# Column groups for sums of squares, and transposes in place of products with the identity

## The reference

```python
def l2norm(x):
    xf = x.astype(jnp.float32)
    return xf * lax.rsqrt(jnp.sum(xf * xf, axis=-1, keepdims=True) + EPS)
...
    o = gated_delta_rule_chunked(heads(l2norm(q)), heads(l2norm(k)), heads(v.astype(jnp.float32)),
                                 heads(g), heads(beta))
```

```python
    d = jnp.where(lower, b[..., :, None] - b[..., None, :] + li[..., None, :], -jnp.inf)
    m_inter = b + m_prev[..., None]
    m_out = jnp.maximum(m_inter, jnp.max(d, axis=-1))
    dw = jnp.exp(d - m_out[..., None])
```

## Time and profile before

| | |
|---|---|
| median of 3 executions | 2449.74 us (2447.25 to 2452.32) |
| the profiled execution | 2448.92 us |
| its span in the profile | 2447.1 us |
| TensorE busy | 2233.5 us (91%) |
| VectorE busy | 1082.5 us (44%) |
| ScalarE busy | 589.0 us (24%) |
| granted TensorE clock, mean | 0.963 of full |
| loads | 266 GB/s on the mean |

### The profile page before, as it was taken

The page is one execution under the profiler, slowest core; times in us unless marked ns, Lnnn a source line. Parts: engine busy times, 40 slices in busy tenths (PEclk is TensorE's granted clock), DMA queues, the critical chain, the costliest instruction groups (busy, mean ns, idle before and its releaser), DMA issues.

```text
span 2447.1 us, 31932 instructions
## 1 busy us (share of the span) xinstructions
PE 2233.5 (91%) x12988; PEld 1448.7 (59%) x12988; DVE 1082.5 (44%) x2393; ACT 589.0 (24%) x1306; POOL 58.4 (2%) x88
## 2 busy tenths in 40 slices
PE   8999999999999999999998997888899999988876
PEld 7888869946865798467764333333568743433332
DVE  4765458883464588543433222222324342222222
ACT  4331513001243220031622211111314422111111
POOL 0010000001000000002000000000002000000000
PEclk9999999999999999999998999999899989999998
DMA  8221244496933645935248999999943469999997
GB/s 305 104 78 69 85 143 170 170 370 210 324 121 106 228 166 206 343 131 172 103 180 360 427 428 427 428 427 428 355 144 111 199 246 428 427 427 427 428 427 309
DMA packets 141343, 650.67 MB, mean 266 GB/s; under 512 B 7018, under 2 KB 13466, under 8 KB 116608
## 3 DMA queue, kind: packets, MB, share of 16 engines
q1 hardware_dynamic: 138768, 641.47, 66.4%
q0 software_dynamic: 2416, 7.02, 1.2%
HBM read 647.16 MB, written 1.31 MB: 265 GB/s over the span
## 4 chain that ended last, share of the span: by engine, by line
PE 63%; DMA 22%; DVE 10%; ACT 3%; issue 1%; DVEq 0%; ACTq 0%
PE ps L106 61%; DMA wring<-in_w_gate 5%; DMA wring<-in_w_up 5%; DMA AR<-in_w_gate 5%; DMA wring<-in_w_down 4%; DVE wring L129 2%; PE ps L109 2%; DMA AR<-in_w_up 2%; DVE AR L125 2%; DVE AR L129 1%; ACT AR L115 1%; ACT L115 1%; ACT HT L115 1%; DVE wring L125 1%; DVE AR L120 1%
## 5 line engine op out<-in xcount | busy, mean ns | idle before, releaser
L106 PE MATMUL ps<-HT,wring 128*128 128x256 f32 (+1 forms) x2848 | 532.3, 345 | 5.7 <-DVE wring L125 4.0
L106 PEld LDWEIGHTS ps<-HT,wring 128*128 128x128 f32 x2848 | 466.6, 193 | 63.5 <-issue 6.6
L106 PE MATMUL ps<-wring,AR 128*32 128x512 f32 (+3 forms) x1312 | 339.1, 616 | 21.9 <-DMA wring<-in_w_down 13.7
L106 PE MATMUL ps<-wring,MN 128*32 128x512 f32 (+1 forms) x1376 | 219.6, 642 | 49.3 <-DMA wring<-in_w_gate 32.0
L115 ACT ACTIVATE AR<-ps 128x128 f32<-128x128 f32 (+6 forms) x234 | 94.6, 404 | 651.9 <-PE ps L106 596.0
L106 PEld LDWEIGHTS ps<-wring,AR 128*32 128x32 f32 (+1 forms) x1312 | 131.8, 152 | 181.5 <-issue 165.5
L141 DVE COPY HT<-ps 128x512 f32<-128x512 f32 x64 | 44.3, 692 | 417.6 <-PE ps L106 417.6
L106 PE MATMUL ps<-AR 128*128 128x128 f32 (+6 forms) x1368 | 195.2, 404 | 15.3 <-DMA AR<-in_w_down 8.2
L106 PEld LDWEIGHTS ps<-wring,MN 128*32 128x32 f32 (+1 forms) x1376 | 62.3, 122 | 196.8 <-issue 105.6
L125 DVE TENSOR_TENSOR AR<-ps,AR 128x512 f32<-128x512 f32 (+4 forms) x200 | 100.5, 503 | 151.5 <-PE ps L106 90.6
L106 PEld LDWEIGHTS ps<-AR 128*128 128x128 f32 (+4 forms) x1368 | 135.9, 175 | 52.0 <-issue 30.5
(11 more groups left out here) (178 smaller groups left out, 2140.9 us busy)
## 6 DMA issues: line engine op xcount, KB each, us to landing
wring<-in_w_up SPq DMA_DIRECT2D x40, 2048.0 KB, 41.8
wring<-in_w_gate SPq DMA_DIRECT2D x38, 2048.0 KB, 44.5
wring<-in_w_down SPq DMA_DIRECT2D x38, 2048.0 KB, 43.2
wring<-in_w_ada SPq DMA_DIRECT2D x24, 2048.0 KB, 11.5
wring<-in_ffn_w_up SPq DMA_DIRECT2D x20, 2048.0 KB, 7.9
AR<-in_w_down SPq DMA_DIRECT2D x20, 2048.0 KB, 46.7
AR<-in_w_gate SPq DMA_DIRECT2D x20, 2048.0 KB, 36.0
wring<-in_w_in SPq DMA_DIRECT2D x18, 2048.0 KB, 9.9
```

The lines of the kernel that those rows point to most:

```text
L106: return Ins(self.eng and self.eng.matmul(out, lhs, rhs, start=start, stop=stop), None)
```

## The change

Three places of the program are edited.

1. The strip is 63 columns wide, and a piece's four matmuls write to the four groups of 32 partitions of the bank, each with 32 weight columns. Head f = 4j + r stands on partition 32r + j; the other rows get only zeros. The roots are then formed over all 128 partitions of `RN`.
2. The roots are transposed whole, two transposes of 128x128. VectorE copies the keys' 16 numbers per token into `rq` in the order of the heads, between its two masks `causal(2)` and `causal(3)`, under the new key `"rk"`. TensorE waits for that, and spreads each key head by transposes of the number repeated 128 times, two a head. The queries' numbers are read later, as before.
3. In the linear memory's `"weigh"` the matmul with the identity is a transpose of the same operand.

```diff
-    parts["strip"] = np.broadcast_to(np.arange(31) == 15, (128, 31))
+    parts["strip"] = np.broadcast_to(np.arange(63) == 31, (128, 63))
...
-                    e.matmul(pss[0:16, 0:256], C("strip", 31)[:, 15 - f:31 - f], SQ[f], f == 0, f == 15).then_inc(done, ("sum", f))
+                    r, j = 32 * (f % 4), f // 4
+                    e.matmul(pss[r:r + 32, 0:256], C("strip", 63)[:, 31 - j:63 - j], SQ[f], j == 0, j == 3).then_inc(done, ("sum", f))
...
             e.wait_ge(vect, "rn")
             for m in range(2):
-                ins = e.transpose(ps[:, m * 16:m * 16 + 16], RN[0:16, tok(m)], IDENT[0:16, 0:16])
+                ins = e.transpose(ps[:, tok(m)], RN[:, tok(m)], IDENT)
             ins.then_inc(done, "rq")
+            rq = sm("rq", 2, 16)
+            e.wait_ge(vect, "rk")
             for h in range(4):
                 ps = bank(e, PA, ("rk", h))
                 for j in range(2):
                     hd = 2 * h + j
-                    ins = e.matmul(ps[:, 256 * j:256 * j + 256], bc(IDENT[0:16, 8 + hd:9 + hd], 128), RN[0:16, :], True, True)
+                    for m in range(2):
+                        ins = e.transpose(ps[:, 256 * j + 128 * m:256 * j + 128 * m + 128], bc(rq[:, m, 8 + hd:9 + hd], 128), IDENT)
                 ins.then_inc(done, ("rk", h))
...
-                            ins = e.matmul(ps[:, k * 128:k * 128 + 128], bc(cb[:, k, 4 * d + hd:4 * d + hd + 1], 128), IDENT, True, True)
+                            ins = e.transpose(ps[:, k * 128:k * 128 + 128], bc(cb[:, k, 4 * d + hd:4 * d + hd + 1], 128), IDENT)
...
-            v.tensor_scalar(RN[0:16, :], PA["squares"][0:16, 0:256], 1e-6, None, ADD).then_inc(done, "squares")
+            v.tensor_scalar(RN, PA["squares"][:, 0:256], 1e-6, None, ADD).then_inc(done, "squares")
             PA.free("squares", (done, "squares"))
-            root_inverse("rn", RN[0:16, :], done)
+            root_inverse("rn", RN, done)
             conv(17)
-            root_step("rn", RN[0:16, :], RN1[0:16, :], RN2[0:16, :], act, done, "rn")
-            for q in range(2, 4):
-                causal(q)
+            root_step("rn", RN, RN1, RN2, act, done, "rn")
+            causal(2)
+            v.wait_ge(mm, "rq")
+            by_head = pair(PB["rq"][:, 0:256]).rearrange("p m (g c) -> p m c g", g=4)
+            rows4 = rq.rearrange("p m (c g) -> p m c g", g=4)
+            v.tensor_copy(rows4[:, :, 2:4, :], by_head[:, :, 2:4, :]).then_inc(done, "rk")
+            causal(3)
```

More of the change, by code:

```diff
@@ L1886, in gdn @@
                 scaled_keys(h)
-            v.wait_ge(mm, "rq")
-            v.tensor_scalar(rq.rearrange("p a b -> p (a b)"), PB["rq"][:, 0:32], 128.0 ** -0.5, None, MUL).then_inc(done, "rq")
+            v.tensor_scalar(rows4[:, :, 0:2, :], by_head[:, :, 0:2, :], 128.0 ** -0.5, None, MUL).then_inc(done, "rq")
             PB.free("rq", (done, "rq"))
@@ L2734, in gdn @@
                 a.activation(DT[q], DT[q], ACT.Exp, scale=-1.0).then_inc(done, ("decay", q))
-            root("rn", RN[0:16, :], RN1[0:16, :], vect, done)
+            root("rn", RN, RN1, vect, done)
             memory_squares(0)
```

## The result

The changed kernel takes 2437.49 us (median of 7), the kernel before 2448.70 (median of 7): a ratio of 0.9957, with a 95% interval of 0.9947 to 0.9967, 11.2 us or 0.43% less. A second series gave 2438.15 beside 2448.31, 10.2 us less. The profiled execution took 2435.96 us, with a span of 2434.2 against 2447.1.

What follows compares the result with a forecast made beforehand. TensorE holds 63% of the chain of waits; TensorE and VectorE are both nearly full at the mixer's roots. 3.7 + 0.25 - 0.2 + 2.7 = 6.45 us less gives 2443.3 us, range 2440.0 to 2447.5.

Steps and rivals of the forecast that it cites:

- The sums: Delta-rule mixer: four grouped matmuls take 0.60 us instead of 1.83; three of four pieces count, 3.7 us at the roots.
- the fourth: Last piece of sums before the roots: its gain only makes TensorE wait longer for the roots.
- the wide operations on VectorE: Roots over 128 partitions instead of 16: priced at nothing, at worst 0.4 us more.
- The keys by transposes: Keys' roots: sixteen transposes replace eight matmuls of 5.44 us; products start after 5.43 us instead of 5.70, gain 0.25 us.
- a sign of failing: At the keys' roots: the prediction fails if TensorE waits longer than 2.5 us for the copy and the keys.
- The clock there: Keys' products: the clock falls as now and returns a few microseconds into them; 0.2 us taken off.
- the transposes would keep it up: Rival, 15%, at the keys' roots: transposes of 128 rows hold the full clock, 1.2 to 1.4 us more gained, 2442.0.
- The rows that I had set against the rule of the Trainium skill: Stretches at 138 to 140 and 1188 to 1190 us: full clock with transposes and waits alone.
- The linear memory: Weights in both layers: groups of four take 0.44 us instead of 0.89; three heads a layer count, 2.7 us.
- What takes the gain to the end: Experts' load stream moves with the stages ahead, so a microsecond won before 1300 is one at the end.
- a new half-clock stretch: Slower rival, 6%: transposes in the linear memory do not hold the clock, six stretches cost 21 us, about 2464.
- a drift that would swallow the gain: Rival, 12%: another engine's chain runs alongside or the half clock returns later; 2 to 4.5 us remain, about 2446.

Runs made afterwards that it cites:

- x10: The kernel before, unchanged, run again for a second profile; its experts' start in layer 0 takes 36.16 us, against 36.40 in the first profile.
- x2: Only the linear memory's weights by transposes, on the kernel before: 2442.58 us beside 2448.31, ratio 0.9976.
- x5: Linear memory's weights by transposes, each done twice, on the kernel before, groups of 0.88 us: ratio 1.0001, median 0.1 us less.
- x6: Linear memory's weights by transposes, each done three times, on the kernel before, groups of 1.31 us: ratio 0.9998, median 0.8 us less.
- x3: Only the keys' roots by sixteen transposes behind VectorE's copy, on the kernel before with 16 rows: 2448.88 us beside 2448.31, ratio 1.0002.
- x4: The changed kernel, unchanged, run again for a second profile: 2438.15 us beside 2448.31 for the kernel before.
- x8: Kernel before with grouped sums, keys' roots by products over 128 rows without copy, linear memory's weights by transposes: 2437.68 us beside 2448.58, ratio 0.9956.
- x1: Only sums in four column groups, keys' roots spread by products over 128 rows, on the kernel before: 2444.77 us beside 2448.31, ratio 0.9988.
- x9: The changed kernel with each linear-memory transpose done twice, groups of 0.88 us: 2445.03 us beside 2448.22 for the kernel before, ratio 0.9985.
- x7: Linear memory's weights by transposes, each done four times, on the kernel before, groups of 1.75 us: ratio 1.0005, median 1.7 us more.

## Why the prediction was wrong

**The sums: right.** 0.57 us a piece (0.60 forecast); three of four count, 3 x 1.26 = 3.8 us (3.7); the fourth went into a longer wait for the roots, and VectorE's wait shrank to 0.53 us (0.5). From the first piece to the roots it was 54.11 us and is 50.39, 3.7 less, so the wide operations on VectorE cost under 0.1 us.

**The keys by transposes: the size agrees by luck.** From the roots to the products it was 5.7 us and is 102.15 - 96.61 = 5.54, a gain of 0.16 (0.25). The copy waits for nothing and takes 0.17 us. But the 5.7 us held half-clock time that need not be there. In the second profile of the kernel before (x10) TensorE spread the roots at full clock and then waited for VectorE:

```profile
101.34 3.69 PE L106 MATMUL ps<-XN,CS 16*128 16x256 f32 x16
106.41 5.43 PE L106 MATMUL ps<-AR 128*128 128x128 f32 x32 [1.37 <-DVE AR L125]
```

The roots were done there at 101.07, so the products start after 5.34 us, as in x2, x5 and x6 (5.33 to 5.34), and the transposes are 0.2 us later than that, the time of the copy. Alone (x3) the edit is not measurable. The changed kernel's second profile (x4) has 5.54 us too:

```profile
98.39 1.96 PE L109 MATMUL ps<-CS,SM 128*128 128x128 f32 x16 [0.50 <-DVE SM L141]
102.87 5.44 PE L106 MATMUL ps<-AR 128*128 128x128 f32 x32 [2.52 <-DVE AR L125]
```

Its waits for the copy and the keys are 3.0 us together, over the 2.5 that the prediction named as a sign of failing; they only take up what the transposes leave at full clock.

**The clock there: right that it falls; that the transposes would keep it up did not come true.** Windows, columns as above, of the changed kernel, then of its second profile, then of x8, where products over 128 rows stand in the transposes' place:

```profile
95.00:110.00 15.00, 11.39 (x64) 10.47 (x64) 13.54 (x29) 0.00 (x0) 0.00 (x0) 0.77 0.39 141
```

```profile
95.00:115.00 20.00, 15.27 (x86) 13.60 (x85) 17.13 (x36) 3.28 (x8) 0.00 (x0) 0.91 0.31 106
```

```profile
95.00:110.00 15.00, 11.96 (x71) 10.39 (x71) 13.60 (x27) 0.24 (x2) 0.00 (x0) 1.00 0.40 141
```

With the transposes the lower clock holds for 0.23 x 15 / 0.5 = 6.9 us in the first profile and 3.6 in the second; with the products, in x1 and in x8, not at all, though the waits in x1 are those of the changed kernel's first profile but for the copy's. In x3 and x9, which have the transposes too, it fell for 3.4 and 6.8 us. The rows that I had set against the rule of the Trainium skill were of stretches with waits of 0.9 to 1.3 us, against up to 1.7 in the first profile here; whether that makes the difference was not tried. That rule of the Trainium skill (TensorE: Matmul & The Clock Gate, Part 4) says that work in transpose mode doesn't count as busy in the same way. The four profiles with transposes agree with its direction, but it isn't the whole: with the 16-row products in their place the clock fell as well, for 3.4 us in x10 and 6.8 in the first profile of the kernel before. That the copy's wait of 0.5 us has no part in it wasn't tried apart.

**The linear memory: right.** 1.53 us a layer (1.35), the wait behind head 1 longer, 1.76 us instead of 1.51. Heads 0, 2 and 3 count. The 0.2 us beyond them are of head 1: its gain of 0.45 was to go into the wait whole, and the wait grew by 0.25 only.

**What failed is the step "What takes the gain to the end".** It said that a microsecond won before 1300 is one at the end. So it put at nothing what the edits do to half-clock time further on. Downstream of the edits the experts' start has a price of its own, which goes with how long TensorE runs at half clock there, and when (in layer 0 13.7 us before, 6.8 after), and the kernel before happened to pay the highest of all lengths tried. That the excess was a gain is luck in this sense. The change shortens the linear memory by 1.5 us, and that lowered the price by 1.77 and 1.20 us. 7.0 + 3.0 = 10.0 us, beside 10.2 and 11.2 in the medians. The 2.9 us that the profiled pair has beyond that are 0.82 before any edit, 1.2 in layer 0's experts and up to the linear memory of layer 1, and 1.7 in layer 1's experts, less 0.8 between 158 and 1137. The second profiles of both kernels (x10 and x4) place them differently: 0.0, 0.7, 0.2 and again 0.8 the other way. In this pair the edits' places give 6.6 us and the two starts 2.7. Most of the 2.9 us is therefore chance, but not surely all: from the first long piece of layer 1 to the end the changed kernel's two profiles and x8 take 437.2 to 437.5 us, and the six of the old length 437.7 to 439.2. No experiment was made on that.

I had the mechanism in view only as a loss (a new half-clock stretch) and as a drift that would swallow the gain. I did not ask what the present kernel pays at each place where the clock is already half, and whether a shift would move that. The earlier trace rows had the sign of it: a granted clock of 0.60 in the ten microseconds ahead of the experts.

**Open.** Why 138.4 us is the dear length, which of the lower prices a start pays, and by what step the clock's fall depends on it, the runs don't settle. And x6 doesn't fit in time: its profile has 2.9 us less at both starts for 1.8 us of added work, which should make it 4 us faster than before; its median is 0.8 faster. Part of it shows in its profile, where the stretch from the first long piece of layer 0 to layer 1's first weights takes 523.1 us, against 521.4 and 521.7 in the kernel before. So what a start saves need not all arrive at the end. The rest is not explained; only the profiled execution shows the starts, and the others may have paid more.

## What to carry to other kernels

In a sum of direct gains, list also the places further on where the clock is at half, with what they cost now, and keep a term of either sign for each: a shift of 1.5 us moved two of them by 3 us here, beside 7 us of direct gains. To test it, lengthen the stage by work that does nothing: if the time doesn't rise in step with it, timing further on has a part in it. And work taken off an engine counts up to the wait that it meets: three of four pieces of sums, three of four heads, and next to nothing of the 3.6 us at the keys' roots.

## What the runs showed of the hardware

Four matmuls of 32 weight columns and 256 moving ones, in four column groups, each with its own wait and signal, take 0.57 us together, against 1.83 for four of 16 columns in one group. The signals did not keep them apart.

The same eight products cost 3.62 us over 128 rows and 3.69 over 16 at full clock (x1, x10); the 5.51 of the first profile are for a part at half clock. The clock stayed at full behind them in both profiles with 128 rows (x1, x8). It fell for 3.4 or 6.8 us in all six with 16 rows (before, x10, x2, x5, x6, x7) and in all four with transposes (changed, x3, x4, x9).

Two profiles of one program agree to 0.3 us at the experts' start, and programs that reach it 4.6 us earlier or 6.0 us later agree as well, while 0.9 us more or 1.5 us less in the stage just ahead changes it by up to 2.9 us. At one and the same length of that stage it can still differ by 1.7 us (x2 against the changed kernel, layer 1).
